# Partial sums in PSUM banks and a re-shared order of work in a six-feed-forward network on one core

## The reference

```python
def _swiglu(x, w_gate, w_up, w_down):
    return (jax.nn.silu(x @ w_gate) * (x @ w_up)) @ w_down      # hidden width 2816

def _layer(x, ...):                                             # first network, twice
    x = x + 0.5 * _swiglu(_rmsnorm(x, ffn1_norm), ffn1_w_gate, ffn1_w_up, ffn1_w_down)
    x = x + mixer(_rmsnorm(x, mix_norm) @ w_in) @ w_out         # gated MLP, short conv, retention
    return x + 0.5 * _swiglu(_rmsnorm(x, ffn2_norm), ffn2_w_gate, ffn2_w_up, ffn2_w_down)

for layer in range(2):                                          # second network
    x = x + mixer(rms_norm(x, ...))      # layer 0: pooling and latent attention; layer 1: linear recurrence
    x = x + mem_cross_attention(rms_norm(x, xa_norm_x[layer]), mem, ...)
    x = x + swiglu(rms_norm(x, ffn_norm[layer]), ffn_w_gate_up[layer], ffn_w_down[layer])
```

## Time and profile before

| | before |
|---|---|
| time, median of 3 runs | 3331.61 us (3331.11 to 3332.47) |
| the profiled execution | 3331.31 us, its span 3330.0 |
| TensorE matmul busy | 3171.0 us, 95% |
| TensorE weight load busy | 2821.3 us, 85% |
| VectorE busy | 2250.1 us, 68% |
| ScalarE busy | 1530.2 us, 46% |
| GpSimd busy | 1197.6 us, 36% |
| mean granted TensorE clock | 0.977 |
| DMA | 322 MB, 97 GB/s |

### The profile page before, as it was taken

The page is one execution under the profiler, slowest core; times in us unless marked ns, Lnnn a source line. Parts: engine busy times, 40 slices in busy tenths (PEclk is TensorE's granted clock), DMA queues, the critical chain, the costliest instruction groups (busy, mean ns, idle before and its releaser), DMA issues. The chain is left out here.

```text
span 3330.0 us, 48176 instructions
## 1 busy us (share of the span) xinstructions
PE 3171.0 (95%) x18984; PEld 2821.3 (85%) x18984; DVE 2250.1 (68%) x2811; ACT 1530.2 (46%) x2253; POOL 1197.6 (36%) x550
## 2 busy tenths in 40 slices
PE   7999999899989999999999999998999899989999
PEld 6999788799968989787898867887999688878988
DVE  7757556865767756576775677558656786477675
ACT  5444433444534534434453445545435385544543
POOL 2443433343334343433434332223443103234332
...
GB/s 116 114 111 96 109 83 79 86 109 108 102 64 108 96 102 89 125 77 69 109 101 95 86 96 70 121 95 83 106 99 112 68 93 123 108 71 114 114 90 77
DMA packets 93295, 322.31 MB, mean 97 GB/s; under 512 B 10512, under 2 KB 14992, under 8 KB 93072
## 3 DMA queue, kind: packets, MB, share of 16 engines
...
...
## 5 line engine op out<-in xcount | busy, mean ns | idle before, releaser
L2970 POOL TENSOR_TENSOR wlo<-raws,whi 128x1024 fp32r<-128x1024 f32 x415 | 1028.1, 2485 | 1656.5 <-ACT whi L1120 1656.2
L1120 ACT ACTIVATE whi<-raws 128x1024 fp32r<-128x1024 f32 x468 | 488.0, 1052 | 473.0 <-PE bank L428 333.6
L424 PE MATMUL bank<-f_hh,whi 128*128 128x512 f32 x904 | 355.5, 393 | 12.7 <-ACT whi L1120 12.7
L425 PE MATMUL bank<-f_hl,whi 128*128 128x512 f32 x904 | 354.7, 392 | 0.0
L2967 POOL TENSOR_TENSOR f_sl<-raws,f_sh 128x512 fp32r<-128x512 f32 x120 | 167.1, 1393 | 455.0 <-ACT f_sh L1231 455.0
L562 PE MATMUL bank<-gxh,whi 128*128 128x256 f32 x960 | 249.4, 291 | 63.5 <-ACT whi L1120 34.0
L424 PE MATMUL bank<-gxh,whi 128*128 128x512 f32 x576 | 229.0, 398 | 31.3 <-DVE gxl L2032 31.0
L562 PE MATMUL bank<-f_th,whi 128*128 128x256 f32 x960 | 245.7, 287 | 10.2 <-ACT f_c L1238 10.2
L1238 ACT ACTIVATE f_c<-bank 128x256 f32<-128x256 f32 x360 | 136.7, 380 | 245.0 <-PE bank L566 233.8
L562 PEld LDWEIGHTS bank<-gxh,whi 128*128 128x128 f32 x960 | 187.5, 195 | 70.4 <-issue 36.3
L563 PE MATMUL bank<-gxl,whi 128*128 128x256 f32 x960 | 246.1, 288 | 0.0
...
## 6 DMA issues: line engine op xcount, KB each, us to landing
...
```

What stands on the lines that cost most here:

```text
L424: pe.matmul(out, seq(hi, k, P), h, start=first and k == 0, stop=False)
L425: pe.matmul(out, seq(hi, k, P), l, start=False, stop=False)
L1120: act.activation(M.whi[r][:, :], M.raw[r][:, :], ACT.Copy).then_inc(*S.tick("hi", u))
L2970: pool.tensor_tensor(M.wlo[r][:, :], M.raw[r][:, :], M.whi[r][:, :].bitcast(F32), ALU.subtract).then_inc(*S.tick("lo", u))
```

## The change

- **Banks.** Banks 4 and 7 become one tensor `banks47`. The SBUF tiles `s13`, `parts` and `gained` go.
- **First weight sum.** ScalarE copies two raw weight blocks into `banks47` (`s13_copy`, new, in `run` and `begin`); VectorE adds the third in place. The second sum reads bank 4. `s13_hi` and `s13_lo` read the banks, and `s13_hi` waits for the second sum.
- **Blocks.** Input blocks are the even tiles and the odd tiles (`BLOCKED`), with the weights' rows in that order from the host; a pair is 2p, 2p+1. `take_gain` writes half a tile to bank 4, `turn_parts` makes its four sums in banks 5 and 6, `turn_hi` and `turn_lo` read them. Three of four pairs are turned within the residual, one step at each tile; the last low part stands behind it.
- **Scaling.** GpSimd multiplies the silu by `R` (`scale`); `gated` waits for that, and the down products are added to `x` straight from the bank: `scaled_part` and the copy of `R` at stage 5 go, and the last half tiles lose their scaling.
- **Low parts.** `hidden_lo` moves from VectorE to GpSimd, whose order in a feed-forward is written out.
- **Tiles.** Feed-forward 0 has four plain tiles in place of two. `begin` of the first quad takes the last plain tile's `silu`, `gated` and `hidden_hi` in its middle. ScalarE makes `silu` of a run's last tile ahead of the second down weight.

The diff, cut to its core (left out: names of semaphores, `PLAIN` with its index, the ring's banks under their new event names, the host's calls):

```diff
-PLAIN = 2
+PLAIN = (4, 2, 2, 2, 2, 2)
+BLOCKED = (0, 2, 4, 6, 1, 3, 5, 7)
...
+        self.bank = [ctx.enter_context(nc.psum_tensor(f"bank{n}", [P, 512], F32)) for n in range(4)]
+        self.banks56, self.banks47 = (ctx.enter_context(nc.psum_tensor(name, [P, 1024], F32)) for name in ("banks56", "banks47"))
+        self.bank += [seq(self.banks47, 0), seq(self.banks56, 0), seq(self.banks56, 1), seq(self.banks47, 1)]
...
+    def take_gain(f, p):
+
+        if p:
+            act.wait_ge(*S.at("turned_parts", f, p - 1))
+        act.activation(bank[4][:, 0:HALF], of_half(M.x, 1, 2 * p), ACT.Copy,
+                       scale=gain_after(M, F_STAGE[f] - 1)(2 * p)).then_inc(*S.tick("gained", f, p))
+
+    def turn_hi(f, p):
+
+        act.wait_ge(*S.at("turned_parts", f, p))
         for n in range(2):
...
+            act.activation(seq(M.f[f]["th"], 2 * p + n), bank[5 + n][:, :], ACT.Copy, scale=-1.0 if n else 1.0).then_inc(
+                *S.tick("turned_hi", f, p))
...
-                if m >= 6:
-                    turn_hi(f, m - 6)
...
+                if m % 2 == 0:
+                    if m:
+                        turn_hi(f, m // 2 - 1)
+                    take_gain(f, m // 2)
...
+        def s13_copy(m):
+            at = U["gate", f, m] % SLOTS * UNIT
+            for kind in ("gate", "up"):
+                u = U[kind, f, m]
+                act.wait_ge(*S.at(f"loaded{u % SLOTS}", u))
+            act.wait_ge(*(S.at("s13_lo", f, m - 1) if m > PLAIN[f] else S.at("turned_lo", f, 3)))
+            act.activation(M.banks47[:, :], M.raws[:, at + SEQ:at + 3 * SEQ], ACT.Copy).then_inc(*S.tick("s13_copy", f, m))
+
...
             u = U["gate", f, m]
...
+            act.wait_ge(*S.at("s2", f, m))
...
+            act.activation(M.whi[u % SLOTS][:, :], M.banks47[:, :], ACT.Copy).then_inc(*S.tick("s13_hi", f, m))
...
+            if first + 1 < end:
+                s13_copy(first + 1)
             for m in range(first, end):
...
+                if m + 2 < end:
+                    s13_copy(m + 2)
...
+        def begin(m, late=None):
             split_hi(U["up", f, m])
+            if late is not None:
+                silu(late)
+            s13_copy(m)
             s13_hi(m)
             s24_hi(m)
             m22_hi(m)
-
-        ahead(("gate", f, 0))
-        if not f:
-            root(i)
-        ahead(("up", f, 0))
+            if late is not None:
+                hidden_hi(late)
+
         if f:
+            tile(0)
+            turn_hi(f, 3)
             root(i)
         else:
+            ahead(("gate", f, 0))
+            root(i)
+            ahead(("up", f, 0))
             take_gain(0, 0)
-            turn_hi(0, 0)
-            take_gain(0, 1)
-            turn_hi(0, 1)
-            take_gain(0, 2)
-        turn_hi(f, 2)
-        take_gain(f, 3)
-        turn_hi(f, 3)
-        silu(0)
-        hidden_hi(0)
-        begin(PLAIN)
-        for c in range(2):
+            for p in range(4):
+                turn_hi(0, p)
+                if p < 3:
+                    take_gain(0, p + 1)
+                if p % 2 == 0:
+                    silu(p // 2)
+                    ahead(("gate", f, p // 2 + 1))
+                else:
+                    hidden_hi(p // 2)
+                    ahead(("up", f, p // 2 + 1))
+        begin(PLAIN[f], PLAIN[f] - 2)
+        for c in range(3):
             run(c)
             ahead(("down", f, c, 0))
+            silu(F_RUNS[c][1] - 1)
             ahead(("down", f, c, 1))
-            silu(F_RUNS[c][1] - 1)
             hidden_hi(F_RUNS[c][1] - 1)
-            for m in range(2, KD - 2):
-                ahead(("down", f, c, m))
-            begin(F_RUNS[c][1])
-        run(2)
-        ahead(("down", f, 2, 0))
-        ahead(("down", f, 2, 1))
-        silu(KF - 1)
-        hidden_hi(KF - 1)
+            if c < 2:
+                for m in range(2, KD - 2):
+                    ahead(("down", f, c, m))
+                begin(F_RUNS[c][1])
         residual(i, [None, None] + [("down", f, 2, m) for m in range(2, KD)])
...
+    def turn_parts(f, p):
...
+        gain, out = gain_after(M, F_STAGE[f] - 1), [of_half(M.banks56, n % 2, n // 2) for n in range(4)]
+        x11, x21, x22, b12 = of_half(M.x, 0, 2 * p), of_half(M.x, 0, 2 * p + 1), of_half(M.x, 1, 2 * p + 1), bank[4][:, 0:HALF]
+        even, odd = gain(2 * p), gain(2 * p + 1)
+        dve.wait_ge(*S.at("gained", f, p))
+        if p:
+            dve.wait_ge(*S.at("turned_lo", f, p - 1))
+        dve.scalar_tensor_tensor(out[0], x11, even, b12, ALU.mult, ALU.subtract).then_inc(*S.tick("turned_parts", f, p, 0))
+        dve.scalar_tensor_tensor(out[1], x22, odd, b12, ALU.mult, ALU.subtract).then_inc(*S.tick("turned_parts", f, p, 1))
+        dve.wait_ge(*S.at("turned_parts", f, p, 1))
+        dve.scalar_tensor_tensor(out[2], x11, even, out[1], ALU.mult, ALU.add).then_inc(*S.tick("turned_parts", f, p, 2))
+        dve.wait_ge(*S.at("turned_parts", f, p, 2))
+        dve.scalar_tensor_tensor(out[3], x21, odd, out[2], ALU.mult, ALU.subtract).then_inc(*S.tick("turned_parts", f, p))
+
+    def turn_lo(f, p):
...
+                dve.wait_ge(*(S.at("xs", i - 1, m) if ends is None else S.at("part_sum", ends, 1, m)))
+            dve.scalar_tensor_tensor(seq(M.x, m), at_bank("xs", i, m)[:, :], scale, seq(M.x, m), ALU.mult,
+                                     ALU.add).then_inc(*S.tick("xs", i, m))
...
             if i + 1 in F_STAGE:
                 f = F_STAGE.index(i + 1)
-                if m >= 6:
-                    turn_lo(f, m - 6)
-                if m in (5, 6):
-                    turn_parts(f, m - 5)
...
+                if m % 2:
+                    turn_parts(f, m // 2)
+                elif m:
+                    turn_lo(f, m // 2 - 1)
...
+            both = M.banks47[:, :].rearrange("p (n c) -> p n c", n=2)
...
-            dve.tensor_tensor(T["s13"][:, :].rearrange("p (n c) -> p n c", n=2),
-                              M.raws[:, at + SEQ:at + 3 * SEQ].rearrange("p (n c) -> p n c", n=2),
-                              weight("gate", m, 0)[:, None, :].to_broadcast([P, 2, SEQ]), ALU.add).then_inc(
+            dve.wait_ge(*S.at("s13_copy", f, m))
+            dve.tensor_tensor(both, both, weight("gate", m, 0)[:, None, :].to_broadcast([P, 2, SEQ]), ALU.add).then_inc(
                 *S.tick("s13", f, m))
             dve.wait_ge(*S.at("s13", f, m))
-            dve.tensor_tensor(bank[5][:, :], seq(T["s13"], 0), weight("up", m, 0), ALU.add).then_inc(*S.tick("s2", f, m))
+            dve.tensor_tensor(bank[5][:, :], bank[4][:, :], weight("up", m, 0), ALU.add).then_inc(*S.tick("s2", f, m))
             dve.wait_ge(*S.at("s2", f, m))
             dve.tensor_tensor(bank[6][:, :], bank[5][:, :], weight("up", m, 1), ALU.add).then_inc(*S.tick("s4", f, m))
...
-            dve.tensor_tensor(M.wlo[r][:, :], T["s13"][:, :], M.whi[r][:, :].bitcast(F32), ALU.subtract).then_inc(
+            dve.tensor_tensor(M.wlo[r][:, :], M.banks47[:, :], M.whi[r][:, :].bitcast(F32), ALU.subtract).then_inc(
...
+            dve.wait_ge(*(S.at("silu", f, m - 1) if m else S.at("rstd", i)))
...
-            dve.wait_ge(*S.at("silu", f, m))
+            dve.wait_ge(*S.at("silu_scaled", f, m))
...
-            dve.wait_ge(*S.at("t", f, m))
-            dve.wait_ge(*S.at("hh", f, m))
-            dve.tensor_tensor(hidden_tile(T["hl"], m), T["u"][:, :], hidden_tile(T["hh"], m).bitcast(F32),
-                              ALU.subtract).then_inc(*S.tick("hidden", f, m))
...
+        def begin(m, late=None):
             sums(m)
             s13_lo(m)
+            if late is not None:
+                gated(late)
...
-        rstd(i)
-        dve.wait_ge(*S.at("rstd", i))
-        for k in range(2 if f else 0, 4):
-            turn_parts(f, k)
-            turn_lo(f, k)
-        gate(0)
-        gated(0)
-        hidden_lo(0)
-        begin(PLAIN)
+            c22(end - 1)
+            gate(end - 1)
+            gated(end - 1)
+
+        if f:
+            turn_lo(f, 3)
+            rstd(i)
+        else:
+            rstd(i)
+            for p in range(4):
+                turn_parts(0, p)
+                if p % 2 == 0:
+                    gate(p // 2)
+                else:
+                    gated(p // 2)
+                turn_lo(0, p)
+        gate(PLAIN[f] - 2)
+        begin(PLAIN[f], PLAIN[f] - 2)
         for c in range(2):
             run(c)
             for m in range(KD):
                 dve.wait_ge(*used("down", f, c, m))
-                scaled_part(f, c, m, at_bank("part", f, c, m)[:, :], M.R)
-                dve.scalar_tensor_tensor(seq(M.x, m), T["u"][:, :], F_SCALE[f], seq(M.x, m), ALU.mult, ALU.add).then_inc(
-                    *S.tick("part_sum", f, c, m))
+                if c:
+                    dve.wait_ge(*S.at("part_sum", f, 0, m))
+                dve.scalar_tensor_tensor(seq(M.x, m), at_bank("part", f, c, m)[:, :], F_SCALE[f], seq(M.x, m), ALU.mult,
```

(46 more changed lines are left out.)

163 lines of the change are left out of this document (49 added, 114 removed).

## The result

The changed kernel takes **3165.12 us** (median of 4 runs, 3164.70 to 3167.81) against 3331.93 (4 runs); the ratio is 0.9501, with a 95% interval of 0.9485 to 0.9518. The profiled execution took 3164.7 us, its span 3163.4.

A forecast was written before the change was run, and what follows sets the result against it. TensorE was taken to bound the kernel, with the winnable time in its stalls at seams and the slow clock after them. Terms summed to 152 us, 3331.6 - 152 = 3180 us, range 3166 to 3214.

The forecast's parts named there:

- feed-forward 0: Start of the kernel's first feed-forward: four plain tiles cover VectorE's turning of the input, -20 us, bounds -16 and -21.
- the way into mixer 1: Residuals from feed-forward into mixer 1: VectorE's work per tile falls from 5.4 to 3.4 us, -12 us in all.
- the ring: Steady feed-forward tiles: a closed chain of steps over four engines takes 10.0 us against TensorE's 10.08, so no loss.
- The first rival: Steady tiles: the chain over four engines takes 10.6 us a tile and drifts, +34 us, 3214; chance 0.20.
- Mixers into feed-forwards: Four ways from mixers into feed-forwards: VectorE is already behind, so spreading turns gains little, -2 us, bounds +4 and -6.
- the starts of feed-forwards 1 to 5: First quads of these feed-forwards: only the last turn is left after the residual, 5 x 10.8 = -54 us.
- the second rival: Residuals into feed-forwards: `acc` sums in odd tiles wait 2.4 us behind GpSimd subtractions, +24 us, 3204; chance 0.15.
- the starts of runs: Starts of runs 2 and 3 of feed-forward tiles: `x` sums no longer wait behind GpSimd, -31 us.
- the ways into mixers 2 and 3: Residuals ahead of these mixers: VectorE catches up except at sine angles or decay rates, -11 and -10 us.
- The third rival: Whole kernel: every small rest goes and the clock does not fall at what is left, -13 us, 3167; chance 0.07.
- The fourth rival: Steady tiles: GpSimd's scaling and `f_sl` are held, tiles take 11.6 us, slower than before at 3356; chance 0.03.
- The speaking-against rule: VectorE operations moved to banks: PSUM's fixed cost is 120 cycles against 58, 0.06 us slower each, 0.2 us per tile.

## Why the prediction was right or wrong

**Right in mechanism.** That VectorE with two SBUF operands waits out GpSimd was the basis of the forecast, and the runs bear it out: the holds come back with turned parts, down scaling or first sum in SBUF, and go with the running sum in bank 7. The Trainium skill's rule (SBUF — State Buffer, Who interferes with whom) agrees with all of them, in both directions: VectorE's 2.85 for 0.68, and GpSimd's 3.39 for 2.4 where it came second. The last test that the forecast named for itself fell its way: in the traces before and after, no VectorE operation with a bank among its inputs takes over 1.3 us. The rule as the forecast worded it is too narrow, though, since an operation over a single SBUF tile can be held too (last section).

**Right in size**: feed-forward 0 (20 against 20.9), the way into mixer 1 (12 against 12.5), steady tiles (nothing against nothing), and the ring, counted at 10.0 and measured at 9.81. The first rival didn't come, by a quarter of a microsecond per tile: 1.3 us more in the ring cost 59 us, so its premise, that the new ring is the danger of this change, was right. The counted margin of 0.08 was too small by 0.19. Round the ring in the trace of the kernel with one more operation, the snapshot is the step that was counted too long: `s24_hi` starts 0.26 us behind the snapshot's start, where 0.38 and a handover were counted.

**The term that failed** is "Mixers into feed-forwards", 2 us with bounds of +4 and -6, measured 13.2. The step was "VectorE is behind from the mixer itself, so spreading the turns only spreads its work". The trace of before shows otherwise: two of the turning operations there took 2.7 us for 0.48 and 0.43, held by GpSimd, 4.4 us at each of four seams. The forecast had written the rule down and applied it to the `x` sums and the weight sums, but didn't look for held operations among the turning ones of the kernel before. TensorE's wait for the last tile fell from 4.6 to between 2.2 and 2.5 us at each of them, and the rest of the 13.2 is slow clock that no longer follows. The test with parts in SBUF brings the holds back, and the one with the old places in banks leaves 0.7 us of the wait of about 4.6 at each of these seams. That is 11.2 of the 15 us by which the sum of the terms was short; with the forecast's 2 us there the time would have been 3176, inside the range.

**The term that was too high** is the starts of feed-forwards 1 to 5: 54 against 45.9. The step "only the last turn is left after the residual, and it ends before `rstd`" left out what stands ahead of both: the last running sums were held 4.2 us (2.85 and 2.71 for 0.68 and 0.69), so the turn, the root and `rstd` came late and the first quads still waited, 8.4 us in all. The versions with bank 7 show it, by giving back 10 us. The collision of the second rival was there, then, but at another operation than it named: not the `acc` sums of odd tiles, where VectorE was first by 0.1 to 0.2 us, but two of the last three sums of each residual, and it cost some 10 us in place of 24.

**Under-sized**: the starts of runs (31 against 34.9), where 3.3 and 1.8 us were booked for run 2 and run 3, and 3.7 and 2.15 came back; the ways into mixers 2 and 3 (21 against 25.2), where the rows that the forecast cites for mixer 3 give 9.7 us in the stretch and 4 off the wait for weights, but 10 in all were booked and what stays was not said; feed-forward 1 into 2 (11.7 against 13.7); the end (0.5 against 1.8). The forecast kept slow clock behind the stalls that are left, and these stretches show 1.00; how much of each term that is wasn't split. The third rival, "more is won", gave 3167 for just this; its chance of 0.07 was too low for a forecast that had rounded most leftovers up, and the range's lower end was set on it with nothing beyond. The fourth rival's price, 176 us above the forecast for tiles of 11.6, was too high: in the kernel with the first sum in SBUF, tiles of 11.64 cost 103 us, since the first tiles of each run are covered by its credit.

**The speaking-against rule** (VectorE: DVE Perf Modes, The TRN2 errata, of the Trainium skill) doesn't show: at 512 and 1024 columns the bank forms take 0.70 and 1.23 us, the SBUF forms beside an idle GpSimd 0.69 and 1.21. Here the measurement decides.

What stays open: why the credit of a run was 4 us in one kernel and less in another wasn't followed.

## What to carry to other kernels

When one rule explains a slow operation, list every operation in the seams that meets its condition before summing, the half-width ones too, and look in the trace for operations of its length that don't meet it; the largest error here was a rule applied to one group and not to its neighbour. A move that lightens the busiest engine can lengthen a ring over four: add up the ring and test it with one more operation, since busy shares (48% on GpSimd) say nothing about it. And an order that is decided by 0.2 us between two engines that share a port should be made safe (an operand in a bank) before it is tuned.

## What the runs showed that had not been expected

The hold works both ways and chains. In the kernel with the first sum in SBUF, a 2.4 us GpSimd operation took 3.39 behind VectorE's sum, and VectorE's next sum 2.79 for 0.7 behind it, so one pair of operands cost 1.56 us in each tile beyond the credit and 103 us in all. And a ScalarE copy of 128x1024 into banks takes 1.02 us, no more than one into SBUF (1.05).

Nor are two SBUF operands the whole condition. In mixer 1 of the changed kernel one VectorE operation over a single SBUF tile takes 0.43 us, and 2.50 when it starts 0.19 us behind a GpSimd subtraction:

```profile
423.29 0.43 DVE L2195 TENSOR_SCALAR m_yh<-m_ga 128x512 fp32r<-128x512 f32 x1
...
426.06 2.50 DVE L2195 TENSOR_SCALAR m_yh<-m_ga 128x512 fp32r<-128x512 f32 x1
...
425.87 2.41 POOL L2954 TENSOR_TENSOR wlo<-raws,whi 128x1024 fp32r<-128x1024 f32 x1 [4.63 <-ACT whi L1119]
```

The kernel before has the same 2.5 us there, and the change left it; what it costs wasn't tested.
